# A hybrid encoder block on one core: token operand loads on another queue, gate buffers doubled, and the steps of decay, attention scalings, linear attention and stores moved by a slot or more

## What is computed

```
h = rmsnorm(x, g_pre)                              # x (1, 2048, 1024) f32
proj = h @ w_in                                    # 1024 -> 7440 columns, split into
(q_a, k_a, v_a, lr_a, z_a, q_b, k_b, v_b, z_b, m_a, m_b) = split_cols(proj)
log_a = log_sigmoid(lr_a @ w_decay_up + b_decay_up) / 16
o_a = gla_mixer(q_a, k_a, v_a, log_a)              # 4 heads, keys 128, values 256, chunks of 64:
        S = S * exp(b_last)[..., None] + einsum('bchk,bhkv...', k * exp(b_last - b), v)
        o = einsum('bchk,bhkv->bchv', q, S)
y_a = (rmsnorm of o_a per head * g_gla * silu(z_a)) @ w_branch_gla
o_b = swa_sink_mixer(rope(q_b), rope(k_b), v_b, sinks)   # 16 heads, 2 kv heads, window of 2 chunks
y_b = (o_b * silu(z_b)) @ w_branch_swa
y = sigmoid(m_a + b) * y_a + sigmoid(m_b + b) * y_b
out = x + rmsnorm(y @ w_out, g_post)
```

## Time and profile before

| | us |
|---|---|
| median of 3 runs | 1937.3 (1936.69 to 1938.97) |
| the profiled execution | 1934.83 |
| its span in the profile | 1933.0 |
| PE busy in it | 1850.8 |
| DVE, POOL, ACT busy | 1252.1, 1020.9, 897.2 |

### The profile page before, as it was taken

One profiled execution on the slowest core, in us unless ns is written; L12 is line 12 of the kernel. 1 busy time (PEld: TensorE's weight loads), 2 busy tenths in 40 slices (PEclk: granted clock), 3 DMA queues, 4 the chain that ended last, 5 costly groups with the idle time before them and its releaser, 6 DMA issues. The chain is left out here.

```text
span 1933.0 us, 31460 instructions
## 1 busy us (share of the span) xinstructions
PE 1850.8 (96%) x11024; PEld 1480.5 (77%) x11024; DVE 1252.1 (65%) x2012; ACT 897.2 (46%) x1962; POOL 1020.9 (53%) x673
## 2 busy tenths in 40 slices
PE   8999999979999999999999999999999999999996
PEld 7877877767777777788877877777777778788785
DVE  6867866757688866546377866655888755453275
ACT  5467555534344454323357555553444553225431
POOL 5634544535345557724434455555455476548755
PEclk9999999989999999999999999999999999999998
DMA  7534386677788877886844365666798786874773
GB/s 275 136 93 132 122 223 173 158 201 216 222 227 242 257 223 251 271 287 223 239 119 135 123 178 160 157 171 155 182 263 245 237 272 210 285 244 150 269 249 119
DMA packets 474463, 391.21 MB, mean 202 GB/s; under 512 B 292835, under 2 KB 365091, under 8 KB 460995
## 3 DMA queue, kind: packets, MB, share of 16 engines
q1 hardware_dynamic: 474307, 389.20, 67.9%
HBM read 256.45 MB, written 132.64 MB: 201 GB/s over the span
## 5 line engine op out<-in xcount | busy, mean ns | idle before, releaser
L1024 PE MATMUL pu<-a_hi,w_hi 128*128 128x512 f32 x1824 | 725.5, 400 | 11.2 <-DVE ct L1862 4.8
L1024 PE MATMUL pu<-a_lo,w_hi 128*128 128x512 f32 x1824 | 712.4, 393 | 0.0
L1024 PE MATMUL pu<-a_hi,w_lo 128*128 128x512 f32 x1824 | 711.4, 392 | 0.4 <-POOL w_lo L2015 0.4
L2015 POOL TENSOR_TENSOR w_lo<-t,w_hi 128x512 fp32r<-128x512 f32 x256 | 361.6, 1421 | 361.7 <-ACT w_hi L1344 361.5
L2015 POOL TENSOR_TENSOR w_lo<-w_raw,w_hi 128x512 fp32r<-128x512 f32 x264 | 398.0, 1519 | 256.7 <-ACT w_hi L1344 256.5
L1024 PEld LDWEIGHTS pu<-a_hi,w_hi 128*128 128x128 f32 x1824 | 345.5, 190 | 108.8 <-issue 33.7
L1024 PEld LDWEIGHTS pu<-a_hi,w_lo 128*128 128x128 f32 x1824 | 345.5, 189 | 74.7 <-POOL w_lo L2015 0.8
L1024 PEld LDWEIGHTS pu<-a_lo,w_hi 128*128 128x128 f32 x1824 | 345.6, 190 | 68.6
L1025 PE MATMUL pu<-a_hi,w_hi 128*128 128x512 f32 x544 | 214.3, 394 | 12.2 <-DVE ct L1876 5.3
L1344 ACT ACTIVATE w_hi<-t 128x512 fp32r<-128x512 f32 x256 | 158.8, 629 | 140.3 <-DVE t L536 59.0
L1025 PE MATMUL pu<-a_lo,w_hi 128*128 128x512 f32 x544 | 213.0, 392 | 0.0
(11 more groups left out here) (177 smaller groups left out, 2304.4 us busy)
## 6 DMA issues: line engine op xcount, KB each, us to landing
w_raw<-in_w SPq DMA_DIRECT2D x81, 1024.0 KB, 6.4
va_d<-ct SPq DMA_DIRECT2D x128, 64.0 KB
qb_d<-ct SPq DMA_DIRECT2D x32, 256.0 KB
zb_d<-ct SPq DMA_DIRECT2D x32, 256.0 KB
q_s<-qb_d SPq DMA_DIRECT2D x32, 256.0 KB, 3.3
z_s<-zb_d SPq DMA_DIRECT2D x32, 256.0 KB, 3.7
gb_d<-gb SPq DMA_DIRECT2D x32, 256.0 KB, 3.2
za_d<-ct SPq DMA_DIRECT2D x128, 64.0 KB
```

The lines of the kernel that those rows point to most:

```text
L1024: return nc.tensor.matmul(dst, weights, moving, start=start, stop=stop, skip_group_check=True)
L2015: TT(flat(w_lo[o.n % NWB][:, :, :]), src, as_f32(flat(w_hi[o.n % NWB][:, :, :])), ALU.subtract) \
```

## The change

- ORDER: group zB 1 goes ahead of qB 2 and qB 3, in both halves (they move 7 slots back).
- load_fill goes from SP's loop to the end of ACT's slot, with its waits, on ACT's own queue. Token sums S2, S3, S1, S4 of the gb operands are loaded (and partly split) one slot later, S3 of the first y operands too.
- z_s and z_g get a second buffer and a semaphore for each. z_s is loaded at first+2 instead of +4, z_g at first+4 instead of +6.
- Linear attention on DVE is one slot later: state at +4, rstd at +7, transpose at +9, ga at +10, its store at +12. kd moves to the end of slot first. PE's and ACT's steps stay where they are.
- Decay: sums and exponential at +5 instead of +6, the store at +6.
- h scalings: HPREP at 101 + 13j, loads 4 slots ahead instead of 5, scalings in two pairs at first−1 and first. The wait for qB 3's finished tiles goes from the load of x_tok to the first load of hx and to ACT's rb copy; x_tok lies in another place.
- y sum jobs at 272 + 20j//3.
- Stores of finished qk, v, m and out tiles one slot earlier, and so the squares and their sums.

The diff, shortened ("..." marks what is left out; eight columns of indentation are removed):

```diff
@@ -24,7 +24,7 @@
 ORDER = ([("v", 0), ("qk", 0), ("v", 1)]
- + [("kvB", 0), ("qB", 0), ("qB", 1), ("zB", 0), ("qB", 2), ("qB", 3), ("zB", 1), ("zB", 2), ("zB", 3)]
+ + [("kvB", 0), ("qB", 0), ("qB", 1), ("zB", 0), ("zB", 1), ("qB", 2), ("qB", 3), ("zB", 2), ("zB", 3)]
@@ -159,10 +159,10 @@
 _order = (("A11", -10, -6, -7), ("A12", -9, -5, -6), ("A21", -5, -2, -5), ("A22", -4, -1, -3),
-          ("S2", -1, 2, -4), ("S3", 0, 3, -2), ("S1", 3, 7, 6), ("S4", 4, 9, -1))
+          ("S2", 0, 3, -4), ("S3", 1, 4, -2), ("S1", 4, 7, 6), ("S4", 5, 9, -1))
...
 _order = (("A12", -20, -16, -33), ("A21", -19, -14, -33), ("S4", -15, -11, -33), ("A11", -10, -5, -6),
-          ("A22", -4, 0, -2), ("S2", -1, 3, -5), ("S3", 0, 4, -1), ("S1", 5, 8, 6))
+          ("A22", -4, 0, -2), ("S2", -1, 3, -5), ("S3", 1, 5, -1), ("S1", 5, 8, 6))
@@ -181,7 +181,7 @@
 SWA = {70 + 4 * n: n for n in range(16)}
-SWA_Z = {first + 4: n for first, n in SWA.items()}
+SWA_Z = {first + 2: n for first, n in SWA.items()}
@@ -191,7 +191,7 @@
 NB = P // TB
-HPREP = {104 + 12 * j: j for j in range(KH)}
+HPREP = {101 + 13 * j: j for j in range(KH)}
@@ -203,7 +203,7 @@
 for _sb in range(NSB):
-    _jobs = [("y", BASE[1] + 5 + 6 * j) for j in range(KH)] if _sb else []
+    _jobs = [("y", BASE[1] + 5 + 20 * j // 3) for j in range(KH)] if _sb else []
@@ -360,7 +360,7 @@
 v_s = [tile(f"v_s{n}", [P, NB, HD], f32, m + (16 * K1, 17 * K1)[n]) for n in range(2)]
-z_s = tile("z_s", [P, 4, P], f32, m + 10 * K1)
+z_s = [tile(f"z_s{n}", [P, 4, P], f32, m + (10 * K1, 18 * K1)[n]) for n in range(2)]
@@ -368,7 +368,7 @@
 d_g = [tile(f"d_g{n}", [P, 2 * P], f32, m + 5 * K1 * n + 4 * K1) for n in range(2)]
-z_g = tile("z_g", [P, 16, TB], f32, m + 10 * K1)
+z_g = [tile(f"z_g{n}", [P, 16, TB], f32, m + (10 * K1, 16 * K1)[n]) for n in range(2)]
@@ -383,7 +383,7 @@
 rb = tile("rb", [P, 2, HT], f32, stage_at)
-x_tok = [tile(f"x_tok{n}", [P, D], f32, stage_at + 4 * K1 + 4 * K1 * n) for n in range(2)]
+x_tok = [tile(f"x_tok{n}", [P, D], f32, stage_at + 8 * K1 + 4 * K1 * n) for n in range(2)]
@@ -602,35 +602,6 @@
-    def load_fill(f):
-        sp.wait_ge(a_lo_d_ok, before + 1)
-        sp.wait_ge(a_lo_p_ok, before + 1)
...
-        go(fill_in[k][:, :, :], rows[q % 2], fill_ok[k])
@@ -700,8 +671,10 @@
             stored(group_no(sb, "zB", 2 * g + 1))
-        sp.wait_ge(gb_ok, n)
-        go(z_s[:, :, :], zb_d[g * 512:(g + 1) * 512, t0:t0 + P].rearrange("(e p) t -> p e t", p=P), swa_z_in)
+        if n >= 2:
+            sp.wait_ge(gb_ok, n - 1)
+        go(z_s[n % 2][:, :, :], zb_d[g * 512:(g + 1) * 512, t0:t0 + P].rearrange("(e p) t -> p e t", p=P),
+           swa_z_in[n % 2])
@@ -737,12 +710,14 @@
         t0 = sb * SB + t * P
-        sp.wait_ge(ga_ok, n)
+        if n >= 2:
+            sp.wait_ge(ga_ok, n - 1)
...
             sp.wait_ge(gb_ok, 16 * (sb + 1))
+            sp.wait_ge(pv_ok, 16 * (sb + 1))
         tg = slice(t0 // TB, (t0 + P) // TB)
-        go(z_g[:, :, :].rearrange("p g t -> p (g t)"),
-           za_d[tg, :, pr * 16:(pr + 1) * 16, :].rearrange("j d g t -> (j d) (g t)"), gla_z_in)
+        go(z_g[n % 2][:, :, :].rearrange("p g t -> p (g t)"),
+           za_d[tg, :, pr * 16:(pr + 1) * 16, :].rearrange("j d g t -> (j d) (g t)"), gla_z_in[n % 2])
@@ -832,11 +807,10 @@
-    fills = {f.load: f for f in FILLS if f.n >= NHEAD}
...
         sb, r = rel(s)
-        if r - 11 in GLA:
-            job = GLA[r - 11]
+        if r - 12 in GLA:
+            job = GLA[r - 12]
@@ -856,13 +830,13 @@
             load_gla_q(sb, GLA[r + 1])
-        if r - 6 in GLA:
-            load_gla_z(sb, GLA[r - 6])
+        if r - 4 in GLA:
+            load_gla_z(sb, GLA[r - 4])
...
             load_swa_v(sb, SWA[r - 1])
-        for g, n in ((step(s, lag), n) for n, lag in ((3, 5), (0, 6), (2, 7), (1, 8))):
+        for g, n in ((step(s, lag), n) for n, lag in ((0, 5), (3, 5), (2, 6), (1, 7))):
@@ -916,8 +890,8 @@
             go(vb_d[t0:t0 + HT, :].rearrange("(t p) c -> p t c", p=P), v_tm[:, :, :], vtm_out)
-        if r - 7 in DECAY:
-            t = DECAY[r - 7]
+        if r - 6 in DECAY:
+            t = DECAY[r - 6]
@@ -955,15 +929,15 @@
                 t = SQUARES[r + 2]
-                if t == 0:
-                    for n in range(4):
-                        sp.wait_ge(f_ok[n], upto(FINISHED if n > 1 else FINISHED_0, group_no(0, "qB", 3)) + 1)
...
                 go(x_tok[t % 2][:, :], x[SB + t * P:SB + (t + 1) * P, :], xt_in[t % 2])
-            if r + 5 in HPREP:
-                j = HPREP[r + 5]
+            if r + 4 in HPREP:
+                j = HPREP[r + 4]
                 sp.wait_ge(x_sq_ok, NT)
+                if j == 0:
+                    for n in range(4):
+                        sp.wait_ge(f_ok[n], upto(FINISHED if n > 1 else FINISHED_0, group_no(0, "qB", 3)) + 1)
@@ -999,8 +973,6 @@
                         go(x_end[half][:, q:8:2, :], xq[1, 2 * half + q], x_end_in[half])
-        if s in fills:
-            load_fill(fills[s])
@@ -1288,8 +1260,8 @@
             decay_logits(NT * sb + DECAY[r])
-        if r - 6 in DECAY:
-            decay_sums(NT * sb + DECAY[r - 6])
+        if r - 5 in DECAY:
+            decay_sums(NT * sb + DECAY[r - 5])
@@ -1362,6 +1334,36 @@
+    def load_fill(f):
+
+        before = f.n - 2
+        act.wait_ge(a_lo_d_ok, before + 1)
+        act.wait_ge(a_lo_p_ok, before + 1)
+        k = (f.n - NHEAD) % 2
+        if f.what == "h":
+            nc.scalar.dma_start(fill_in[k][:, :, :], h_d[f.name]).then_inc(fill_ok[k], 16)
+            return
+        if f.name == ("A12" if (f.sb, f.what) == (0, "y") else "A11"):
+            if f.what == "gb":
+                if f.sb == 0:
+                    act.wait_ge(h_out, 16 * 7 * KH)
+                act.wait_ge(gb_out, 16 * 16 * (f.sb + 1))
+                act.wait_ge(gs_out, 16 * 4 * jobs_done(f.sb, "gb"))
+            elif f.what == "ga":
+                act.wait_ge(ga_out, 16 * NB * 16 * (f.sb + 1))
+            else:
+                for c in range(4):
+                    act.wait_ge(ct_out[c], stores_before(c, group_no(f.sb, "yA", 3) + 1))
+        if f.name[0] == "S":
+            act.wait_ge(gs_out, 16 * 4 * jobs_done(f.sb, f.what))
+            nc.scalar.dma_start(fill_in[k][:, :, :], sums_d[f.sb, f.what][f.name]).then_inc(fill_ok[k], 16)
+            return
+        src = rows_d[f.what]
+        q = QUARTERS.index(f.name)
+        t0 = f.sb * SB + q // 2 * HT
+        rows = src[:, t0:t0 + HT].rearrange("(j o p) t -> o p j t", o=2, p=P)
+        nc.scalar.dma_start(fill_in[k][:, :, :], rows[q % 2]).then_inc(fill_ok[k], 16)
+
@@ -1411,8 +1414,8 @@
                 A(pm[2 + half][:, :], tab[:, 0, half * HT:(half + 1) * HT], ACT.Copy).then_inc(cos_ok, 1)
-        if r - 6 in DECAY:
-            n = NT * sb + DECAY[r - 6]
+        if r - 5 in DECAY:
+            n = NT * sb + DECAY[r - 5]
@@ -1439,6 +1442,9 @@
             act.wait_ge(rb_ok, 3 + RB[r])
+            if RB[r] == 0:
+                for n in range(4):
+                    act.wait_ge(f_ok[n], upto(FINISHED if n > 1 else FINISHED_0, group_no(0, "qB", 3)) + 1)
@@ -1565,13 +1571,15 @@
         for k, tile_n in enumerate(TILE_ORDER):
-            g = step(s, 5 + k)
+            g = step(s, 4 + k)
...
             split_fill(SPLIT_AT[s])
+        if s in fills:
+            load_fill(fills[s])
@@ -1802,34 +1810,27 @@
             dve.wait_ge(pv_ok, n + 1)
-            dve.wait_ge(swa_z_in, 16 * (n + 1))
+            dve.wait_ge(swa_z_in[n % 2], 16 * (n // 2 + 1))
...
                pm_all[:, 1:5, 0:P].rearrange("p i (e q) -> p i e q", e=4),
-               z_s[:, :, :].rearrange("p e (i q) -> p i e q", i=NB), ALU.mult).then_inc(gb_ok, 1)
+               z_s[n % 2][:, :, :].rearrange("p e (i q) -> p i e q", i=NB), ALU.mult).then_inc(gb_ok, 1)
...
             rstd(r_sm[:, 9, :], r_sm[:, 2, :], r_sm[:, 5, :], rstd_ok)
-        if r - 8 in GLA:
-            n = 16 * sb + GLA[r - 8]
+        if r - 9 in GLA:
+            n = 16 * sb + GLA[r - 9]
...
             V.transpose(o_n[:, :], o_n[:, :]).then_inc(o_t_ok, 1)
-        if r + 1 in GLA:
-            n = 16 * sb + GLA[r + 1]
-            b = n % 2
-            dve.wait_ge(gla_in[b], (n // 2 + 1) * 16 * 3)
-            V.transpose(v_g[b][:, :], v_g[b][:, :]).then_inc(kd_ok, 1)
-            link(V.transpose(k_g[b][:, :], k_g[b][:, :]))
-            TT(k_g[b][:, :], k_g[b][:, :], d_g[b][:, :], ALU.mult).then_inc(kd_ok, 1)
-        if r - 6 in GLA:
-            n = 16 * sb + GLA[r - 6]
+        if r - 7 in GLA:
+            n = 16 * sb + GLA[r - 7]
...
             rstd(pm[0][:, 0:2], pm[0][:, 2:4], sm[:, 5, :], o_r_ok)
-        if r - 3 in GLA:
-            n = 16 * sb + GLA[r - 3]
+        if r - 4 in GLA:
+            n = 16 * sb + GLA[r - 4]
@@ -1925,13 +1926,13 @@
                 first = {v: k for k, v in HPREP.items()}[j]
-                if r in range(first - 3, first + 1):
+                if r in (first - 1, first):
...
                     dve.wait_ge(rb_sb_ok, 2)
```

(27 more changed lines are left out.)

28 lines of the change are left out of this document (3 added, 25 removed).

## The result

The changed kernel takes 1923.45 us (median of 4 runs, 1919.97 to 1927.8), the kernel before beside it 1938.13 us; the ratio is 0.9923 with a 95% interval of 0.9895 to 0.9951. It is faster by 14.7 us, where 38 were forecast, and it lies 1.5 us above the forecast range. In the profiled executions, 1934.83 and 1919.97 us, the spans are 1933.0 and 1918.0 us.

The account below looks back on a forecast made before the run. TensorE was taken as the bound, busy 1850.8 of 1933.0 us. Terms summed to −37.4 us, from 1934.83 to 1897.4 us for the profiled execution; with the median 2.5 us higher, 1899 us was forecast, range 1882 to 1922.

Parts of the forecast that it names:

- the price of a stall with its dip: TensorE (PE): stalls over 2 us halve its clock afterwards; each such dip was counted as 1.7 us beyond the stall.
- Decay: PE's four waits for ScalarE's decay exponential, two per half, shrink or go with one slot earlier: −16.9 us, bounds −12 and −19.5.
- h scalings at 104, 116 and 128: Attention stalls near 366 us, 416 us and the next: +3.9, −6.4 and −4.5 us from pairing and spacing by 13.
- Y sums: Second half, slot 295: last stores land late, so ACT's soft, v_tm and PE wait: +5.9 us, bounds 0 and +11.
- Last h block and linear attention: Moved h block avoids stalls near 510 us, −5.9; linear attention one slot on, allowance +2, bounds 0 and +10.
- kd arrives late: Rival, chance 0.07: DVE exceeds 0.5 us of room, each of 32 linear attention jobs stops PE; 1949 us.
- Token operand loads: SP's waits in load_fill go, so stalls at 1580 us and its twin near 743 us go: −5.4 and −2 us.
- ACT's waits at nothing: load_fill's waits for a_lo on ACT, at most 4 us, covered by w_hi's 5 slots ahead: no cost, else up to +25.
- The sign that I had named for a failure: On ACT: waits for fills showing up ahead of p1 and w_hi would mean the prediction fails; no size given.
- Gate load and rotary wait: Slots 76 and 78 and second half: z_s stall goes, −7.1, rotary wait comes, +4.0; together −3.7, bounds −9.5 and 0.
- half of it comes back: Rival, chance 0.20: moved DVE work delays rotary, hx at 116, y sums and decay places, giving 1918 us.
- The case of loads that bring nothing: Rival, chance 0.08: stores wait for DMA engines, not SP, so 12 us of gain stay away; 1911 us.

Follow-up runs that it names:

- the experiment: Changed kernel with one part undone: decay sums and exponential at +6, store at +7, 1938.66 us; or y sum jobs at 272+6j, 1918.30 us.
- the first trace: First profiled execution of the changed kernel, nothing further edited: 1919.97 us, span 1918.0 us.
- the second: Trace of the changed kernel run again without an edit, as reference for the follow-up runs: median 1921.82 us, ratio to before 0.9932.

## Why the forecast was wrong

**Right.** What bounds the kernel, and the price of a stall with its dip at the place itself. Decay: 16.9 forecast, 16.8 by the experiment, though 19.9 to 21.8 in the first trace, so the close agreement is in part luck. h scalings at 104, 116 and 128: −7.0 forecast, −7.2 in the trace. Stall at 104: +3.9 against +4.5. Y sums: +5.9 against +5.6 in the trace and 3.5 by the experiment. Squares: −4.4 against −3.2 in the trace; no run undoes them.

**Wrong.** The step that failed is the sum over the other parts: each removed stall was counted as won, and what stood behind it on DVE, POOL and ACT was put at nothing or too low. Apart from decay the parts were to bring 20.5 us; without decay's part the changed kernel is 2.8 us slower than the kernel before. Term by term:

- *Last h block and linear attention, −5.9 + 2 forecast; +2.9 in the first trace, +7.1 in the second.* Two readings failed. The stalls at 142, 150 and 414 were not from h scalings but from kd and states standing ahead of ct; moving kd to the slot's end took them away and put waits for kd in their place. And I read the room of 0.5 us at kd from one slot (571.57 and 572.04) in which DVE had only column sums besides. At slots 143, 151, 407 and 415, z tiles (L1908, L1904), at 143 an h sum too, stand ahead of kd, each 0.7 us or more, and the room is negative. The rival "kd arrives late" named this mechanism; nine jobs of 32 waited, 9.7 us in all. The worst slot's rows were wanted, not a typical one's.
- *Token operand loads, −7.4 forecast, +0.9 in the first trace.* The stalls at 212 and 476 went, but putting back the queue or the gb load slots, each by itself, doesn't bring them back, so "the tile came late because SP's store did" isn't shown. Behind it stood POOL's and DVE's backlog of splits and column sums, 3.3 us and a dip three slots on.
- *ACT's waits at nothing.* I named w_hi and p1 as what is queued behind ACT's new waits and forgot the squares for rstd. In the changed kernel the later rstd covers them; without that they cost 3.2 us and a dip, twice. The sign that I had named for a failure is in the changed kernel's list of waits, and in neither the kernel before's nor that of the loads on SP:

```profile
ACT w_hi L1316 <- POOL a_lo L2032: 18.6, 5, 4.0
```

- *Gate load and rotary wait, −3.7 forecast, +1.6 in the first trace.* The stall at 78 went (−7.0, forecast −7.1), but by the order of the groups and not for the reason given: the load waited for the store that it reads, and not for x_tok's. The rotary wait was 4.5 and 3.7 us instead of 2.3 and 1.8 (my own terms, 6.6 less 4, give 2.6 and not 2.3). The estimate spread DVE's mean idle share over four slots, yet its rows from 240 us to the turn's end at 255 us show one gap, of 0.13 us. Among them is one rotary instruction of 2.41 us (L1702, at 243.28).

- *Slot 132, 0 forecast, +3.7 in the first trace.* It isn't in the second trace of the same kernel, which loses more at slot 143 instead. I had looked at the slots where the stalls were, and not at all four h blocks; whether the spacing makes it stays open.

Why DVE is late in linear attention's stretch is shown only in part. One trace pair speaks for slack lent by PE's own stalls: with the stall at 132, PE waits 2.2 us for kd at 143, without it 3.2. But in the second half no h block runs, PE's stall ahead of the stretch is longer than in the kernel before (3.65 at 340 for 2.41 at 342), and the waits for kd are there all the same. There it is kd's place in the slot.

Of the rivals, "half of it comes back", 1918 us, was the nearest, with DVE as its cause; but of its four places only the rotary wait came out worse than forecast, and most of the loss lay at places that it didn't name. The case of loads that bring nothing happened too, inside it, but for the squares, whose share came. PE's share in linear attention's stretch, above 99% in the forecast, is 98.8% (197.57 of 200 us). Two cases say the same: at 476 and 479, and at 205 and 215, a stall removed from a chain of busy engines uncovers the next.
